# Joined kernel: seams mended, and the mLSTM projections read x times gains without the norm's root

## What is computed

```python
mod = c_act @ ada_w[layer] + ada_b[layer]          # c_act = silu(c): shift, scale, gate, twice
h = modulate(rms_norm(x, attn_norm[layer]), sh_a, sc_a)
x = x + gt_a * mix
...
return rms_norm(x, final_norm)                     # end of the first block
# mLSTM layer of the second block
proj = rms_norm_2(h, norm_g) @ w_in                # (512 x 1024) @ (1024 x 4104)
qk, v, o, z, gates = jnp.split(proj, ...)
qk = jax.nn.silu(causal_depthwise_conv(qk, conv_w))
gates = gates + b_gate
...
h = num / jnp.maximum(jnp.abs(den), jnp.exp(-m_s))[..., None]
ht = jax.nn.sigmoid(o) * ht
ht = rms_norm_2(ht, hnorm_g)
y = ht * jax.nn.silu(z)
```

## Time and profile before

| | us |
|---|---|
| median of 3 runs | 2116.03 |
| lowest and highest | 2113.04, 2121.13 |
| the profiled execution | 2119.31 |
| its span, first to last instruction | 2117.5 |
| mean granted TensorE clock | 0.958 of full |

### The profile page before, as it was taken

The page is one execution under the profiler, slowest core; times in us unless marked ns, Lnnn a source line. Parts: engine busy times, 40 slices in busy tenths (PEclk is TensorE's granted clock), DMA queues, the critical chain, the costliest instruction groups (busy, mean ns, idle before and its releaser), DMA issues.

```text
span 2117.5 us, 24340 instructions
## 1 busy us (share of the span) xinstructions
PE 1979.0 (93%) x9300; PEld 1632.0 (77%) x9300; DVE 1173.3 (55%) x2049; ACT 847.5 (40%) x1319; POOL 0.2 (0%) x4
## 2 busy tenths in 40 slices
PE   1999989999998999889989999999999999999999
PEld 0877667888886887789977888888787877777877
DVE  8557846665657465556545333435663455755554
ACT  3226723232223533356633231323444444657343
POOL 0000000000000000000000000000000000000000
PEclk9999998999999979589999999999999999999999
DMA  9661053546554222000022222222121232232021
GB/s 355 209 208 41 1 198 140 202 177 216 179 198 159 99 80 80 0 1 2 1 85 86 92 90 97 99 99 99 60 100 60 80 125 79 81 120 80 1 90 60
DMA packets 42216, 223.85 MB, mean 106 GB/s; under 512 B 4444, under 2 KB 5212, under 8 KB 23694
## 3 DMA queue, kind: packets, MB, share of 16 engines
q1 hardware_dynamic: 41602, 222.25, 29.5%
q10 hardware_dynamic: 524, 0.41, 0.1%
HBM read 219.45 MB, written 3.19 MB: 105 GB/s over the span
## 4 chain that ended last, share of the span: by engine, by line
PE 82%; DVE 8%; DMA 4%; ACT 4%; issue 2%; SPq 0%; DVEq 0%; ACTq 0%
PE bank L422 22%; PE bank L423 22%; PE bank L424 22%; PE bank L1564 3%; PE bank L1535 2%; DMA raw<-wts_d 2%; PE bank L1525 1%; DMA adab<-ada_d 1%; ACT wH L403 1%; PE bank L1526 1%; PE bank L2736 1%; DVE wL L408 1%; DMA ada<-ada_d 1%; DVE tmp L532 1%; PE bank L741 1%
## 5 line engine op out<-in xcount | busy, mean ns | idle before, releaser
L422 PE MATMUL bank<-hH,wH 128*128 128x512 f32 x1328 | 530.2, 399 | 59.5 <-DVE hL L541 37.0
L423 PE MATMUL bank<-hL,wH 128*128 128x512 f32 x1328 | 524.8, 395 | 0.0
L424 PE MATMUL bank<-hH,wL 128*128 128x512 f32 x1328 | 524.2, 395 | 0.0
L422 PEld LDWEIGHTS bank<-hH,wH 128*128 128x128 f32 x1328 | 254.7, 192 | 120.8 <-issue 59.3
L1006 ACT ACTIVATE wH<-raw 128x2048 fp32r<-128x2048 f32 x64 | 122.7, 1917 | 468.8 <-PE bank L424 468.8
L408 DVE TENSOR_TENSOR wL<-raw,wH 128x2048 fp32r<-128x2048 f32 x76 | 174.0, 2290 | 228.0 <-ACT wH L403 227.7
L423 PEld LDWEIGHTS bank<-hL,wH 128*128 128x128 f32 x1328 | 254.7, 192 | 53.7 <-issue 1.0
L424 PEld LDWEIGHTS bank<-hH,wL 128*128 128x128 f32 x1328 | 254.2, 191 | 54.1
L1050 DVE TENSOR_TENSOR wL<-raw,wH 128x2048 fp32r<-128x2048 f32 x64 | 146.5, 2289 | 225.8 <-ACT wH L1006 225.8
L403 ACT ACTIVATE wH<-raw 128x2048 fp32r<-128x2048 f32 x76 | 145.3, 1911 | 246.8 <-PE bank L424 208.4
L422 PE MATMUL bank<-aH,wH 128*128 128x512 f32 x512 | 199.2, 389 | 0.0
(11 more groups left out here) (367 smaller groups left out, 2633.4 us busy)
## 6 DMA issues: line engine op xcount, KB each, us to landing
raw<-wts_d SPq DMA_DIRECT2D x140, 1024.0 KB, 4.9
adab<-ada_d SPq DMA_DIRECT2D x96, 512.0 KB, 4.4
ada<-ada_d SPq DMA_DIRECT2D x4, 2048.0 KB, 22.4
bt<-bias_rows SPq DMA_DIRECT2D x1, 4096.0 KB, 13.0
x<-x_d SPq DMA_DIRECT2D x1, 2048.0 KB, 9.8
peF<-ple_d SPq DMA_DIRECT2D x2, 1024.0 KB, 5.6
out_d<-x SPq DMA_DIRECT2D x4, 512.0 KB, 2.7
pF<-p_d SPq DMA_DIRECT2D x2, 512.0 KB, 3.5
```

The costliest lines, as they stand in the source:

```text
L422: pe.matmul(o, l[0], r[0], start=start, stop=False)
L423: pe.matmul(o, l[0], r[1], start=False, stop=False)
L424: return pe.matmul(o, l[1], r[0], start=False, stop=stop)
```

## The change

**adaLN rows** have four slots instead of two (`ada_slot`: three in `adab`, one in `adac`), `ada0` lies in the region of the bias, halves 14 and 15 are loaded ahead of the reload of `cb`, and `mod_cols` for rows 16 to 39 moves ahead of the differential attention. The halves of a_in are permuted so that the first halves of tiles 0 and 1 come first.

```diff
+    a_in = tiles(i["a_w_in"][0])[[0, 2, 1, 3, *range(4, 12)]]
...
-    t("ada0", [P, 8, D], "h")
+    t("ada0", [P, 8, D], "bias")
...
-    t("adab", [P, 2, D], "ada")
-    t("cb", [P, D], "ada", 8 * K)
+    t("adab", [P, 3, D], "ada")
+    t("adac", [P, D], "misc")
+    t("cb", [P, D], "ada", 12 * K)
...
+            if j < 4:
+                sp.wait_ge(ada_in[j], 16)
+            else:
+                sp.wait_ge(ada_used, j - 3)
+            sp.dma_start(ada_slot(j), d["ada"][k]).then_inc(ada_in[j % 4], 16)
...
+            for n in (16, 17):
+                for k in range(4):
+                    ada_load(sp, 40 + 4 * (n - 16) + k)
+                load_half(sp, n)
```

```diff
+            for e in range(2):
+                for t in (1, 0):
+                    sp.dma_start(sb[f"ada{t}"][:, 4 * e:4 * e + 4, :],
+                                 d["ada"][8 * t + 4 * e:8 * t + 4 * e + 4].rearrange("k p n -> p k n"))\
+                        .then_inc(ada_in[2 * e + 1 - t], 16)
+                    if (e, t) == (0, 1):
+                        sp.dma_start(x[:, :, :], d["x"]).then_inc(x_in, 16)
+                    if (e, t) == (0, 0):
+                        load_half(sp, 0)
+                        load_half(sp, 1)
+            load_half(sp, 2)
...
+                if n >= 1:
+                    load_half(sp, n + 2)
                 for k in range(max(3 * n - 1, 0), min(3 * n + 2, 24)):
                     ada_load(sp, 16 + k)
+                if n == 2:
+                    sp.wait_ge(f_out, 16)
+                    sp.wait_ge(ada_pre, 16)
+                    sp.dma_start(sb["bt"][:, :, :], skewed).then_inc(bt_in, 16)
+            load_half(sp, 14)
...
-            act.activation(sb["ce"][:, :], sb["cb"][:, :], ACT.Exp, scale=-1.0).then_inc(first_e, 1)
+            act.activation(sb["ce"][:, :], sb["cb"][:, :], ACT.Sigmoid).then_inc(first_e, 1)
+            act.preload_act_table_set(EXP_LN)
...
+            hi(act, 0)
+            act.wait_ge(ada_pre, 8)
+            apply_act(act, 0, lambda c: mod(c), chunks=range(0, 4))
+            hi(act, 1)
...
+            hi(act, 2)
+            act.wait_ge(ada_pre, 16)
+            apply_act(act, 0, lambda c: mod(c), chunks=range(4, KC))
...
+            for e in range(2):
+                for t in (1, 0):
...
+                    dve.wait_ge(ada_in[2 * e + 1 - t], 16)
+                    for c in range(4 * e, 4 * e + 4):
+                        a = sb[f"ada{t}"][:, c, :]
+                        gain, first = (col("attn_norm", c), start[:, c:c + 1]) if t else (1.0, col("ada_b", c))
+                        dve.tensor_tensor_reduce(a, a, cb, gain, first, ALU.mult, ALU.add, mod(8 * t + c))\
+                            .then_inc(ada_pre, 1)
+                lo(dve, 2 * e)
+                dve.wait_ge(ada_pre, 8 * e + 8)
+                apply_dve(dve, 0, 0, lambda c: mod(8 + c), lambda c: mod(c), chunks=range(4 * e, 4 * e + 4))
+                if e == 0:
+                    lo(dve, 1)
...
+            pe.wait_ge(w_hi, 1)
+            fill(pe, bank[:, 3, :], 10)
+            for n, (a, j) in enumerate(((0, 0), (1, 0), (0, 1), (1, 1))):
...
+                    pe.wait_ge(f_row, 2)
+                pe.wait_ge(w_lo, n + 1)
+                if n == 0:
+                    first_chunk(pe, 0, lambda m: wpart(0, 0, m * P, P), 1)
+                for kk in range(1 if n == 0 else 0, 4):
+                    k = 4 * j + kk
+                    pe.wait_ge(h_lo, k + 1)
```

```diff
+        def first_chunk(pe, b0, w, count):
+            pe.wait_ge(h_hi, count)
+            for m in range(4):
+                pe.matmul(bank[:, b0 + m, :], w(m)[0], hH[:, 0, :], start=True, stop=False)
+                pe.matmul(bank[:, b0 + m, :], w(m)[1], hH[:, 0, :], start=False, stop=False)
+            pe.wait_ge(h_lo, count)
+            for m in range(4):
+                pe.matmul(bank[:, b0 + m, :], w(m)[0], hL[:, 0, :], start=False, stop=False)
...
+        def fill(pe, o, n):
+            for _ in range(n):
+                pe.matmul(o[:, 0:P], ident[:, :], ident[:, :], start=True, stop=True)
...
+            if s in (1, 2, 3):
+                fill(pe, bank[:, 4 * (next_a % 2) + 3, :], 13)
...
             if s == 0:
-                pe.wait_ge(acc_free[0], 4 * 14)
+                pe.wait_ge(acc_free[0], 4 * 13 + 2)
...
-                hi(act, n + 3)
+                if a < 26:
+                    hi(act, n + 3)
...
+            hi(act, N_C0 + 1)
...
-                    hi(act, N_B1 + 1)
-                    gelu_act(act, 1, N_B1)
+                    gelu_act(act, 1, N_B1, lambda e: hi(e, N_B1 + 1))
```

```diff
-                pe.wait_ge(ks_lo, i + 1)
+                pe.wait_ge(ks_lo, max(i + 1, 2))
                 for n, part, c, b, r in parts(u):
-                    pe.matmul(bank[:, u % 2, part], q_stack(4 * g + r, i), ksH[:, b, g, 0:w], start=True, stop=False)
+                    more = min(part.stop + P, T) if i == 0 else part.stop
+                    pe.matmul(bank[:, u % 2, part.start:more], q_stack(4 * g + r, i),
+                              ksH[:, b, g, 0:more - part.start], start=True, stop=False)
...
-                    pe.wait_ge(kc_ev, 1)
                     pe.wait_ge(acc_free[1], 4 * 14)
                     pe.wait_ge(acc_free[0], 4 * 15)
+                    fill(pe, bank[:, 0, :], 5)
+                    pe.wait_ge(kc_ev, 1)
...
+                    pe.matmul(bank[:, 6 + hd % 2, (hd // 2) * 32:(hd // 2) * 32 + 160], q_stack(hd, i),
+                              sb["kcH"][:, :, :].rearrange("p r n -> p (r n)")[:, g * 32:g * 32 + 160],
+                              start=True, stop=False)
...
+                if i == 0:
+                    fill(pe, bank[:, 3, :], 6)
...
+                if i + 1 == NT:
+                    fill(pe, bank[:, 0, :], 9)
...
+            fill(pe, bank[:, 7, :], 3)
...
+            fill(pe, bank[:, 0, :], 3)
```

```diff
-            stats_two_pe(pe)
...
+            pe.wait_ge(sq_sum, SUM0[4] + 15)
+            pe.matmul(bank[:, 1, :], sb["mean"][:, :], sq_slot2(0), start=True, stop=True).then_inc(stat_mm, 1)
+            pe.matmul(bank[:, 0, :], sb["mean"][:, :], sq_slot(0), start=True, stop=True).then_inc(stat_mm, 1)
...
+                act.activation(hH[:, c, :], x[:, c, :], ACT.Copy, scale=mod(c)).then_inc(h_hi, 1)
...
+                dve.scalar_tensor_tensor(out=hL[:, c, :], in0=x[:, c, :], scalar=mod(c),
+                                         in1=hH[:, c, :].bitcast(F32), op0=ALU.mult, op1=ALU.subtract).then_inc(h_lo, 1)
...
-            apply_act(act, 5, None, mid)
+            mid(act)
+            sq_two_act(act, xw_evac(45), LATE)
+            hi(act, N_MI + 2)
+            root_act(act, 4, bank[:, 1, :], rstd[:, :], one[:, 0:1])
...
+            x_gains_dve(dve, range(6, KC))
+            mid(dve)
+            sq_two_dve(dve, LATE)
+            sq_two_end(dve)
...
+        def m_root_pe(pe):
+            pe.wait_ge(rstd_done, 5)
+            pe.wait_ge(acc_free[1], 4 * 23 + 1)
+            for i in range(NT):
+                last = pe.matmul(bank[:, 4, i:i + 1], rstd[:, i * P:(i + 1) * P], ident[:, 0:1], start=True, stop=True)
+            last.then_inc(rc_mm, 1)
...
+        def m_pre_dve(dve):
+            dve.wait_ge(gg_mm, 1)
+            for j in range(2):
+                p = slice(32 * j, 32 * j + 4)
+                dve.tensor_tensor(rows[:, j, :], bank[p, 0, :], rstd[p, :], ALU.mult).then_inc(r_dve, 1)
...
+            for c in range(4 * (a - 47), 4 * (a - 46)):
+                act.wait_ge(acc_free[a % 2], 4 * (a // 2) + c % 4 + 1)
+                act.activation(qkM[:, c, :], xc[:, c % 2, 3:T + 3], ACT.Copy, scale=col("conv", 24 + c)).then_inc(cv_0, 1)
+                if c % 4:
                     conv_sigmoid(act, c - 1)
-            if a == 48:
-                conv_sigmoid(act, 7)
...
+                o, freed = evac(dve, a, c % 4)
+                dve.tensor_tensor(xc[:, c % 2, 3:T + 3], o, rstd[:, :], ALU.mult).then_inc(freed, 1)
...
+            for c in range(c0, c0 + 4):
+                if c > c0:
+                    conv_silu(dve, c - 1)
+                if c < c0 + 3:
+                    scaled(c + 1)
...
+                for n, j in enumerate((2, 1, 0)):
                     if n == 0:
-                        dve.tensor_scalar(y, src, tap, None, ALU.mult).then_inc(cv, 1)
+                        dve.wait_ge(cv_0, c + 1)
...
-                hi(act, n + 2)
+                if a > 47:
+                    hi(act, n + 2)
+                if a == 48:
+                    m_root_act(act)
                 if a == 49:
                     m_pre_act(act)
...
-                                   o.rearrange("p (h d) -> p h d", h=2), ACT.Copy).then_inc(freed, 1)
+                                   o.rearrange("p (h d) -> p h d", h=2), ACT.Copy, scale=rho[:, m:m + 1])\
+                        .then_inc(freed, 1)
...
+                if a == 49:
+                    m_pre_dve(dve)
                 lo(dve, n + 2)
...
```

(9 more changed lines are left out.)

304 lines of the change are left out of this document (147 added, 157 removed).

## The result

The changed kernel takes **2048.27 us** (median of 3 runs, 2046.73 to 2049.1) against 2116.03: ratio 0.9675, 95% interval 0.9644 to 0.9707. Five further runs of it gave a median of 2048.0. The forecast was 2038, range 2017 to 2068: the time lies in the range, 10 us above the forecast. The profiled execution took 2049.1 us, 70.2 less than that of before; the forecast's sum was 78.9. In a second trace of the changed kernel (after_again, part 3) the lead was 75.8. The kernel before has one trace, so its own spread is not in any of these figures.

What follows compares the result with a forecast made beforehand. TensorE, busy 1979.0 of 2117.5 us, bounds the kernel: time comes only from its 138 idle us and slow matmuls. Terms sum to 78.9; 2119.3 less that is 2040.4, by the median 2037; forecast 2038, range 2017 to 2068.

Steps and rivals of the forecast that it cites:

- Start: Before the first large matmul: new load order and product in two parts bring it near 34 us; 16.8 us gained.
- the warm-up: Matmuls ahead of the first large one: save half of some 3 us at the low clock, put at 0.8 us.
- Rival C: Slower than before: weight halves of a_in starve, their loads behind ada rows and 4 MB of bias; chance 0.02.
- Late rows: Ahead of the first scores: four slots end VectorE's wait for the last ada row; 2.1 us gained.
- halves: Gaps of 1.77 and 2.01 us at lo(14) and lo(15): both halves loaded ahead; 3.8 us gained.
- norm seams: Three seams between stages: shorter waits, earlier first chunks, fills holding the clock; 7.7, 6.0 and 2.2 us gained.
- second compression: Gap of 2.52 us ended by gx behind a split: gx first gives 0.8, plus half the low-clock stretch; 1.5 us.
- Rival A: The fills do not hold the clock, at the seams or in NSA: 30 us lost, 2068 us; chance 0.12.
- NSA: NSA attention: matmuls at the upper clock, first weights 3.1 us earlier, wide scores nearly free; 17 us, bounds 3 and 24.
- mLSTM seam: Tile 47 follows at once without the norm: net 10.2, less 1.7 and 1.1 ahead of tiles 49 and 50; 7.4 us.
- Rival B: VectorE becomes the bound where TensorE gets faster: conv stalls, NSA's first block, start 3 us later; 2051 us; chance 0.14.
- Rival E: Narrow matmuls keep the spacing of their weight load whatever the clock: NSA's term 3, 2052 us; chance 0.01.

Runs made afterwards that it cites:

- after_again: The changed kernel once more, unaltered, with a second trace: 2048.0 us (2043.52 to 2051.06).
- part 3: The follow-up that traced the unaltered changed kernel again and compared the length of the NSA attention across traces: 2048.0 us.
- no_fill: The changed kernel without any filling matmul (start, norm seams, NSA): 2056.86 us, ratio 0.9725.
- tiles_in_turn: The changed kernel with its first two tiles in turn instead of interleaved, halves in that order: 2054.66 us.
- over eight: Eight traces of the changed kernel and variants in which nothing of the NSA attention was edited; that part's mean length was 237.6 us.
- undo_gains: The changed kernel with the mLSTM part taken back alone, x multiplied by gain and root before the projections: 2052.88 us, ratio 0.9694.

## Why the prediction was right, and where it missed

The time lies in the range, and most of the steps came as they were told. The forecast itself is 10 us too low; two steps are wrong by mechanism, and in two more the clock's chance behaviour is part of the number.

**Start (16.8; 16.1).** First large matmul at 34.71 (34.0 worked out), root at 28.57 (27.9), no stall at the second four chunks. The 0.8 for the warm-up is not half of the 3 us that the step names; it was 0.9 by pairs, and 1.4 against no_fill. The run tiles_in_turn shows that the interleaving carries 12.8 of it. Rival C (starving halves) did not occur: no gap in the four tiles.

**Late rows, halves, norm seams (2.1, 3.8, 7.7, 6.0, 2.2; 3.0, 5.7, 8.3, 6.2, 2.6).** Every one was within 1 us but the halves, where the stretch of low clock behind the second gap (1.5) was in the trace of before and not in my term. The late row's number is luck in part: no gap was to be left there, and 1.12 and 1.11 are, so that 0.8 us by the gaps and 2.2 by the clock make up the 3.0. The second compression (3.1, not 1.5) is luck too: the gap left is 1.83, as worked out, and my term had half of the low-clock stretch, while the clock held in this trace; in after_again it fell there and took 1.6 back. Rival A is refuted: the clock was 1.00 behind the fills of the three seams and of NSA's end, and no_fill shows them worth what they were priced at, seam 2 excepted. Only behind the fills ahead of NSA's first scores did it fall.

**NSA (17; 9.1 in the trace, 12.1 over eight).** This is one of the two terms that failed. The step said that behind the first weights TensorE would run at the upper level, "I take 12 of the possible 15.6", with VectorE's chain as what is left. It did so for 11 us; then a wait for one evacuation, queued on VectorE behind work for the next block, let the clock fall for 20 us. That gap had been in the trace of before as one of 1.76 us, ended by the same evacuation (`oB`), at a time when the clock was down already and could not fall:

```profile
884.21 1.11 PE L1564 MATMUL bank<-vB,ptB 128*128 128x65 f32 x4 [1.76 <-DVE oB L1655]
```

I had counted gaps by length and not asked what each would do once the clock was up. In five of the eight traces the clock fell ahead of the first scores besides, which the step did not have either. The widened scores did cost next to nothing, but not by the line that the step draws: between 124 columns at 0.109 and 512 at 0.226, 256 come to 0.149 and not 0.12. In the trace after, a wide and a narrow one together took 0.23 us at a clock of 1.00 (827.03 to 827.26). The lower bound of 3 and the upper of 24 hold both values.

**mLSTM seam (7.4; 2.2, or 1.3 against undo_gains).** The other. Gross gain right; the stall ahead of tile 49 was put at 1.7 and was 3 (4.1 with the root's four matmuls, which took 0.8 and not 0.4), since a chunk on VectorE takes 4.23 us and not 3.76: the exposed sigmoid (0.70) is in no instruction's duration. Behind it the clock fell (3.0 in this trace, 1.5 in after_again), which I had at nothing. Tile 50's 1.1 was right (1.18).

**Tile 55's second half (-1.8).** The gap is 2.08 where before has 1.96, with the same cause; the clock fell behind the one and not behind the other. It was not in the sum and could not have been: the 13 traces of the changed kernel and its variants all have a gap of 1.96 to 2.7 us there, and the clock held in five.

**Rival B**, VectorE as the bound where TensorE gets faster (2051), is the nearest of the rivals to what happened, in time and in two of its three places; but what made its stalls dear was the clock behind them, and the start was not late. Its 0.14 was too little against 0.66. **Rival E:** the scores' spacing was 0.11 us a matmul at 1.00 and 0.21 at 0.50 again, so the spacing of narrow matmuls does follow the clock.
